# A hybrid decoder step: another order of the projection's column tiles and a recurrence period of five units

## What is computed

```python
def layer(x, st_h, st_conv, st_gla, reset_first, p):
    h = rmsnorm(x, p['norm_pre'][0])
    x = x + 0.5 * rmsnorm(swiglu(h, ...[0]), p['norm_post'][0])
    h = rmsnorm(x, p['norm_pre'][1])
    m, h_last, new_conv, S_fin = mixer(h, st_h, st_conv, st_gla, reset_first, p)
    x = x + rmsnorm(m, p['norm_post'][1])
    h = rmsnorm(x, p['norm_pre'][2])
    x = x + 0.5 * rmsnorm(swiglu(h, ...[1]), p['norm_post'][2])
```

```python
    xl, yl, q, k, v, g, gd = jnp.split(h @ p['w_in'], IN_SPLITS, axis=-1)
    xc, new_conv = causal_conv(xl, st_conv, p['conv_w'], p['conv_b'])      # width 4
    r = sigmoid(blockdiag(xc, wa) + ba);  i = sigmoid(blockdiag(xc, wx) + bx)
    log_a = -8 * r * softplus(-lam);      a = exp(log_a)
    h[t] = a[t] * h[t-1] + sqrt(-expm1(2 * log_a[t])) * i[t] * xc[t]
    lru_out = rmsnorm(h * gelu(yl), p['lru_norm'])
    gk = log_sigmoid(gd @ w_gate + b_gate) / 16       # forget gates, per key channel
    o  = gated linear attention of q, k, v with exp(cumsum(gk)), in chunks
    gla_out = rmsnorm(o, p['gla_norm']) * silu(g)
    out = concatenate([lru_out, gla_out]) @ p['w_out']
```

## Time and profile before

| | |
|---|---|
| median of 3 runs | 2257.86 us (2255.24 to 2258.48) |
| profiled execution, its own time | 2258.48 us |
| its span in the trace | 2256.7 us |
| TensorE busy | 2227.5 us |
| VectorE busy | 1371.7 us |
| ScalarE busy | 1172.6 us |
| GpSimd busy | 734.5 us |
| read from HBM | 343.12 MB |

### The profile page before, as it was taken

The page is one execution under the profiler, slowest core; times in us unless marked ns, Lnnn a source line. Parts: engine busy times, 40 slices in busy tenths (PEclk is TensorE's granted clock), DMA queues, the critical chain, the costliest instruction groups (busy, mean ns, idle before and its releaser), DMA issues.

```text
span 2256.7 us, 40446 instructions
## 1 busy us (share of the span) xinstructions
PE 2227.5 (99%) x16890; PEld 2191.0 (97%) x16890; DVE 1371.7 (61%) x1787; ACT 1172.6 (52%) x1824; POOL 734.5 (33%) x793
## 2 busy tenths in 40 slices
PE   8999999999999999999999999999999999999998
PEld 8999999999999899999999999999899998999998
DVE  6554757647885457745474557676479755475454
ACT  6534547535674345544454445574376653454433
POOL 3112512516544225521251124143264523252112
PEclk9999999999999999999999999999899999999999
DMA  6555555445544355555555555554355443655554
GB/s 211 167 160 161 167 168 158 141 120 160 160 151 131 118 174 155 167 165 164 164 161 165 165 165 160 168 158 133 102 178 150 143 139 105 184 160 161 163 165 129
DMA packets 102261, 350.62 MB, mean 155 GB/s; under 512 B 11296, under 2 KB 16416, under 8 KB 102080
## 3 DMA queue, kind: packets, MB, share of 16 engines
q1 hardware_dynamic: 100848, 346.76, 50.5%
q10 hardware_dynamic: 1232, 1.27, 0.2%
HBM read 343.12 MB, written 4.87 MB: 154 GB/s over the span
## 4 chain that ended last, share of the span: by engine, by line
PE 93%; DVE 5%; POOL 1%; ACT 1%; issue 1%; DMA 0%; SPq 0%; DVEq 0%; ACTq 0%; POOLq 0%
PE psD L445 86%; DVE wl L1032 2%; DVE hl L1084 1%; PE psM L587 1%; PE psM L563 1%; POOL inv L1467 1%; DVE diag L1046 1%; PE psM L647 1%; PE psM L636 0%; PE psS L451 0%; PE psM L665 0%; DVE x L1074 0%; PE psS L686 0%; DVE y L1070 0%; PE psS L689 0%
## 5 line engine op out<-in xcount | busy, mean ns | idle before, releaser
L445 PE MATMUL psD<-hh,wh 128*128 128x288 f32 x3712 | 1113.7, 300 | 8.1 <-DVE hl L1084 3.0
L445 PE MATMUL psD<-hl,wh 128*128 128x288 f32 x3712 | 1101.2, 297 | 0.0
L445 PE MATMUL psD<-hh,wl 128*128 128x288 f32 x3712 | 1097.7, 296 | 0.0
L1032 DVE TENSOR_TENSOR wl<-raw,wh 128x1024 fp32r<-128x1024 f32 (+1 forms) x656 | 818.5, 1248 | 130.8 <-ACT wh L756 130.8
L756 ACT ACTIVATE wh<-raw 128x1024 fp32r<-128x1024 f32 (+1 forms) x656 | 672.9, 1028 | 145.5 <-DMA raw<-in_w_gu 52.4
L445 PEld LDWEIGHTS psD<-hh,wh 128*128 128x128 f32 x3712 | 701.9, 189 | 17.3 <-issue 8.3
L445 PEld LDWEIGHTS psD<-hh,wl 128*128 128x128 f32 x3712 | 704.9, 190 | 0.0
L445 PEld LDWEIGHTS psD<-hl,wh 128*128 128x128 f32 x3712 | 703.0, 189 | 0.8
L1682 POOL TENSOR_TENSOR hidl<-hid,hidh 128x288 fp32r<-128x288 f32 x176 | 210.0, 1193 | 952.0 <-ACT hidh L985 952.0
L445 PE MATMUL psD<-hidh,wh 128*128 128x288 f32 x1408 | 417.6, 297 | 0.0
L445 PE MATMUL psD<-hidl,wh 128*128 128x288 f32 x1408 | 415.5, 295 | 0.0
(11 more groups left out here) (191 smaller groups left out, 1455.4 us busy)
## 6 DMA issues: line engine op xcount, KB each, us to landing
raw<-in_w_gu SPq DMA_DIRECT2D x352, 512.0 KB, 3.6
raw<-in_w_d SPq DMA_DIRECT2D x128, 448.0 KB, 3.2
raw<-in_w_in SPq DMA_DIRECT2D x80, 512.0 KB, 3.6
raw<-in_w_d SPq DMA_DIRECT2D x64, 512.0 KB, 3.6
raw<-in_w_out SPq DMA_DIRECT2D x32, 512.0 KB, 3.6
gates<-in_w_ax SPq DMA_DIRECT2D x4, 512.0 KB, 4.9
S<-in_st_gla SPq DMA_DIRECT2D x4, 512.0 KB, 4.6
out_gla_s<-S SPq DMA_DIRECT2D x4, 512.0 KB, 5.2
```

The costliest lines, as they stand in the source:

```text
L445: mm = e.matmul(out, w[:, kt * P:(kt + 1) * P], t[:, kt, :], start=(kt == 0 and part == 0), stop=(kt == KT - 1 and part == 2))
L1032: e.tensor_tensor(wl[u % RING][:, 0:width], raw[u % RING][:, 0:width], wh[u % RING][:, 0:width].bitcast(F32), ALU.subtract).then_inc(lo_re ...
```

## The change

Three lines differ. The order of the projection's column tiles changes, and the period of the recurrence goes from four to five units; the end constant follows from it. The host packs the weights by the same table, so that each unit reads its weights from the same place in the stream as before.

```diff
-W_IN_ORDER = [0, 4, 8, 9, 1, 5, 10, 11, 2, 6, 7, 16, 3, 17, 18, 19, 12, 13, 14, 15]
-R_PERIOD = 4
+W_IN_ORDER = [0, 8, 9, 10, 11, 1, 4, 5, 6, 7, 2, 16, 17, 18, 19, 3, 12, 13, 14, 15]
+R_PERIOD = 5
 R_END = R_PERIOD * (LT - 1) + 7
```

## The result

The changed kernel takes 2287.53 us (median of 4 runs, 2285.91 to 2288.94) against 2256.62 for the kernel before in the runs beside it: ratio 1.0136, 95% interval 1.0118 to 1.0153, 30.9 us slower. I had forecast 2278, 19.7 us slower, with a range up to 2287. The tail's mechanism is the one forecast; the price is half as high again, because two other steps of the forecast failed: it had a small gain inside the projection, and nothing for TensorE's clock.

What follows compares the result with a forecast made beforehand. TensorE, busy 99% of the span, was taken to bound the kernel. Tail delays of 2 x 5.0 and 2 x 5.7 us less 1.7 gained made +19.7 on 2258.48, forecast as 2278 us, range 2265 to 2287.

Steps and rivals of the forecast that it cites:

- The tail's mechanism: Behind the projection: ScalarE's added loads delay VectorE and the keys; TensorE 5.0 us late in group 0's mixers, 5.7 in group 1's.
- Reading the bound: Whole kernel: TensorE busy 99%, so order gains only where it waits; the gates' waits for xc total 3.7 us.
- rival 3: Group 1's projections: VectorE becomes the bound, waits for xc up to 10.8 us, 2287 with the tail; chance 0.08.
- Inside the projection: Gate matmuls of group 1's mixers: the wait for xc changes, between 3.7 us gained and 1.7 lost in all.
- 1.7 us gained: Group 1's gates: waits for xc fall from 3.7 us in sum to 1.0 in each of two mixers.
- The chain on ScalarE: Behind the projection: 20.8 us from first SiLU to the exponentials' load, with seven loads, four new; 6.6 or 7.3 us late.
- VectorE's wait at the ratio: At slot 21 VectorE waits for the last tile's logarithms, about 6 us, once in each mixer.
- the stall at unit 26: TensorE waits about 2.3 us for unit 26's weight subtraction, in each of four mixers.
- the keys: At L616 TensorE waits about 2.7 us for the first chunk's keys, four times, after a slack of 1.6 us.
- Fewer loads: ScalarE's function sets are shared, saving one load a mixer (2273 us) or two (2268); chance 0.14.
- double-priced switches: On ScalarE a switch costs about twice its load, 36 us more, 2314 us; chance 0.01.
- The absorbing lookahead: Behind the projection: weights prepared units ahead hide the tail, 2255 to 2257 us; chance 0.10.

Runs made afterwards that it cites:

- Experiment 9: The changed kernel with VectorE's first softplus step moved from slot 10 to slot 13: 2286.07 us, ratio 1.0127.
- 10: The kernel before with TensorE's last gates moved from slot 15 to 16: 2256.32 us, ratio 0.9991.
- 11: The kernel before with VectorE's softplus steps at slots 14 and 15 instead of 10 and 14: 2255.89 us, ratio 0.9993.
- 1: The changed kernel with the old order of tiles and the new period of five: 2286.07 us, ratio 1.0126.
- 2: The kernel before with only its last tiles later, convolutions at slots 0, 4, 9 and 15: 2284.42 us, ratio 1.0117.
- 3: The changed kernel with each mixer's last tile using Identity for its table functions except GELU, without the logarithms' load: 2259.83 us, ratio 1.0009.
- experiment 4: The changed kernel with the output gate's SiLU ahead of the last tile's sigmoids, one table load fewer a mixer: 2280.68 us, ratio 1.0104.
- 7: The changed kernel with the first chunk's value and key transposes at attention slot 9 instead of 8: 2282.19 us, ratio 1.0100.
- 8: The changed kernel with 16 needless matmuls before TensorE's wait for the keys in each mixer: 2285.06 us, ratio 1.0112.
- 12: The kernel before with softplus steps at slots 14 and 15 and the last gates at slot 16: 2256.85 us, ratio 0.9994.
- third group: The last of three groups of kernels, each run on one chip beside the kernel before, whose median in this group was 2258.95 us.
- 5: The kernel before with three needless table loads at slots 20 to 22 of each mixer, nothing moved: 2270.30 us, ratio 1.0053.
- 6: The kernel before with convolutions at slots 0, 5, 9 and 13, the last tile one slot later: 2266.43 us, ratio 1.0043.

## Why the prediction was right in kind and too low

**Reading the bound.** Right: the change had at most 3.7 us to win, and its effect lay behind the projection. The measured time, 2287.53 us, lies just above the upper end of the range, which was rival 3's figure. That nearness is luck: rival 3 needed waits for xc of 10.8 us, and they are 4.5.

**Inside the projection.** This step failed. The term "1.7 us gained" was wrong in sign: 0.8 us were lost. I took 1.0 us of remaining wait in each of group 1's mixers, near the lower end; it was 2.27 us, at the third gates. I had named slot 10, where convolution, softplus and the boundary's operand meet, as rival 3 and weighed it too lightly; only the third gates wait, though, and not the fourth. Experiment 9 shows that this slot makes the wait; 9, 10 and 11 show that a wait taken from a late VectorE comes back in part one to five units later.

**The chain on ScalarE.** Right: seven loads, four of them new, the counts exact (25, 4 and 4). Its length was 21.3 us against 20.8 summed. The 0.5 us is the overlap of activations: I took the weight rounding at 0.95 us, from start to start in the earlier trace rows, and in front of a load it takes its full 1.05; the same happens at the other loads. VectorE's wait at the ratio was 6.0 us against "about 6", the stall at unit 26 2.3 against 2.3 (with 0.4 at unit 25, where I had none), the keys 2.6 against 2.7. Tail in all: 23.1 us against 21.4. Experiments 1, 2 and 3 show that the period, in it the last tile, in it the loads of its table functions, are the cause; experiment 4 shows the price of one load. A switch cost its 1.28 us, the lost overlap of 0.1 and nothing behind it, as read from the earlier trace rows: in the new timeline the GELU load starts at 399.21, 0.01 us after the root's Exp ends, and GELU itself at 400.51, 0.02 us after the load.

**The missing term.** This is the larger failure. No term of the sum stood for TensorE's clock, and no reason was given for leaving it at nothing. The profile has 174 half-clock matmuls in 12 stretches against 118 in 8, and each costs 0.11 us: 56 x 0.11 = 6.2 us, about the 6.6 of the table's last two rows. With the 2.5 us of the projection and the 1.7 of the tail these make the 10.8 us between the 19.7 forecast and the table's 30.5. Over the profiles, those of the kernels that carry the whole tail or most of it (the change, experiments 1, 2, 4, 7, 8, 9) have 152 to 188 such matmuls, those without it (the kernel before, 3, 10, 11, 12) 96 to 147.

One profile a kernel is little, but the mean granted clock was noted for every run. It is 0.986 to 0.988 in the changed kernel's five runs and 0.989 to 0.993 in the 23 of the kernel before in the third group; by kernel, the means are 0.985 to 0.989 with the tail and 0.991 without it (experiments 5 and 6: 0.988 and 0.989). Within those 23 runs the time goes with the clock: the four at 0.993 took 2254.4 to 2254.9 us, the seven at 0.989 took 2260.5 to 2263.0, 1.65 us for each 0.001. So most of the scatter between single runs is half clock; and by this slope the fall from 0.9906 to 0.9868 is worth 6.3 us, an estimate that agrees with the 6.6.

That the tail's waits bring the stretches is likely by this; it is not shown. Filling one wait (experiment 8) moved the stretch and did not remove it, and a stretch can come near `wout` without any wait ahead. In the ten microseconds before the one at 494.1 us TensorE nowhere waits more than 0.03 us; the last 3.7 of them are the attention's small matmuls, which both kernels have. The ten microseconds before it, then the stretch itself, in the changed kernel:

```profile
484.10:494.10 10.00, 10.00 (x102) 9.77 (x103) 4.79 (x8) 4.18 (x6) 1.24 (x1) 1.00 0.57 159
494.10:500.90 6.80, 6.80 (x42) 6.47 (x39) 0.00 (x0) 0.00 (x0) 0.00 (x0) 0.50 0.00 0
```

So the 3.2 us of the table's last row may owe nothing to the change: whether a stretch comes at `wout`, and which of several waits one follows, differs from profile to profile, and stays open.

**Rivals.** Fewer loads and double-priced switches are out by the load counts and the gaps. The absorbing lookahead is real, but smaller than the chain: it took 1.6 us of delay at the keys in every mixer, and in experiment 3 it hid nearly all.

## What to carry to other kernels

When a period grows, look where the last step lands, not at the average spacing: here three slots moved one tile's sigmoid, logarithm and exponential between the SiLUs of the next stage, and each alternation cost a table load on an engine that others wait for in order. Follow the chain from there over each engine's queue, and subtract the slack at each meeting point once; that sum was right to 8%. Then leave room for TensorE's clock: in three of the changed kernel's four mixers one of the tail's two waits of 2.1 to 2.5 us was followed by 11 to 15 matmuls at half clock, up to 1.6 us more.

## What the runs showed of the hardware

The half clock was the surprise: after 9.7 us at a granted clock of 1.00 and a wait of 2.46 us, the clock was 0.53 for 3.5 us. A stretch that falls in front of a later wait costs nothing, since that wait only gets shorter by it (third mixer: 1.2 instead of 2.7 us at the keys). And a stretch also comes where TensorE has not waited, as at 494 us behind the attention's small matmuls. The same wait can be followed by one or not: behind the broadcast of 1.55 us at `wout` one follows at 523.9 us in the changed kernel, and none at 516.0 us in the kernel before.

A table load does not wait for its activation's input. With ScalarE idle the load ran at 377.86 us, and the SiLU it was for started at 384.34 after 5.19 us of waiting, so this load cost nothing. In the first mixer's tail, from 384.34 to 405.68 us, ScalarE had no such idleness left, and there each load counted.
